# Norms without shift: the product with the root moves to GpSimd in odd rows, and the weight into the copy and the low half

## The reference, cut to what matters

```python
def rms_norm(x, g):
    xf = x.astype(jnp.float32)
    y = xf * lax.rsqrt(jnp.mean(xf * xf, axis=-1, keepdims=True) + RMS_EPS)
    return y.astype(x.dtype) * g.astype(x.dtype)
...
h = h + dilated_attention_mixer(rms_norm(h, attn_norm[j]), positions, ...)
h = h + swiglu(rms_norm(h, ffn_norm[i]), ffn_w_in[i], ffn_w_out[i])
h = h + mlstm_mixer(rms_norm(h, mlstm_norm[j]), ...)
```

## Time and profile before

| | |
|---|---|
| median of 3 runs | 2984.96 us |
| lowest, highest | 2984.22, 2986.41 us |
| profiled execution | span 2983.2 us, 43523 instructions |
| busy | TensorE 97%, VectorE 67%, ScalarE 40%, GpSimd 12% |
| mean granted TensorE clock | 0.992 of full |

### The profile page before, as it was taken

The page is one execution under the profiler, slowest core; times in us unless marked ns, Lnnn a source line. Parts: engine busy times, 40 slices in busy tenths (PEclk is TensorE's granted clock), DMA queues, the critical chain, the costliest instruction groups (busy, mean ns, idle before and its releaser), DMA issues.

```text
span 2983.2 us, 43523 instructions
## 1 busy us (share of the span) xinstructions
PE 2888.3 (97%) x18080; PEld 2524.0 (85%) x18080; DVE 2004.9 (67%) x3284; ACT 1202.5 (40%) x1993; POOL 349.9 (12%) x542
## 2 busy tenths in 40 slices
PE   7999999989999999999999999999999999998998
PEld 7999998889997778888866888888888888877898
DVE  7776887668655557777745677777777777554665
ACT  5444544554444444223314533223243222443543
POOL 0000001000022220000131100011010000243000
PEclk9999999999999999999999999999999999999999
DMA  7544675347655424555473255553535555465453
GB/s 241 168 159 152 216 229 190 120 161 234 204 125 81 72 64 147 157 167 169 132 190 107 80 168 163 169 165 124 170 120 164 168 163 169 117 96 86 142 184 128
DMA packets 362277, 451.85 MB, mean 151 GB/s; under 512 B 12656, under 2 KB 332432, under 8 KB 362080
## 3 DMA queue, kind: packets, MB, share of 16 engines
q1 hardware_dynamic: 326976, 329.83, 34.1%
q0 software_dynamic: 34944, 118.65, 16.9%
q10 hardware_dynamic: 160, 0.59, 0.1%
HBM read 438.60 MB, written 1.05 MB: 147 GB/s over the span
## 4 chain that ended last, share of the span: by engine, by line
PE 79%; DVE 12%; ACT 5%; DMA 2%; issue 1%; POOL 1%; DVEq 0%; SPq 0%; ACTq 0%
PE ps L1352 23%; PE ps L1354 23%; PE ps L1353 23%; DVE lo L1932 4%; PE ps L1530 1%; ACT hi L1602 1%; PE ps L1373 1%; PE ps L1517 1%; DVE NB L1963 1%; DMA NB<-in_na_rpb 1%; PE ps L1375 1%; PE ps L1374 1%; DVE MX L2008 1%; PE ps L1505 1%; DVE XN L1969 1%
## 5 line engine op out<-in xcount | busy, mean ns | idle before, releaser
L1352 PE MATMUL ps<-XN,hi 128*128 128x256 f32 (+1 forms) x3184 | 1048.8, 329 | 32.9 <-DVE XN L1949 9.9
L1353 PE MATMUL ps<-XN,hi 128*128 128x256 f32 (+1 forms) x3184 | 1029.9, 323 | 0.0
L1354 PE MATMUL ps<-XN,lo 128*128 128x256 f32 (+1 forms) x3184 | 1029.6, 323 | 0.0
L1932 DVE TENSOR_TENSOR lo<-raw,hi 128x1024 fp32r<-128x1024 f32 (+1 forms) x626 | 739.2, 1221 | 250.6 <-ACT hi L1602 245.4
L1602 ACT ACTIVATE hi<-raw 128x1024 fp32r<-128x1024 f32 (+1 forms) x626 | 620.6, 1040 | 443.5 <-PE ps L1354 440.7
L1352 PEld LDWEIGHTS ps<-XN,hi 128*128 128x128 f32 x3184 | 610.6, 192 | 106.6 <-issue 17.4
L1354 PEld LDWEIGHTS ps<-XN,lo 128*128 128x128 f32 x3184 | 610.8, 192 | 46.1
L1353 PEld LDWEIGHTS ps<-XN,hi 128*128 128x128 f32 x3184 | 611.2, 192 | 44.8
L2008 DVE CUSTOM_DVE_ANT_0 MX<-MW,C 128x1024 bf16<-128x1024 f32 x384 | 477.2, 1243 | 130.7 <-DMA MW<-in_mod_w 123.8
L1352 PE MATMUL ps<-H,hi 128*128 128x512 f32 (+1 forms) x1072 | 380.2, 355 | 0.0
L1353 PE MATMUL ps<-H,hi 128*128 128x512 f32 (+1 forms) x1072 | 379.7, 354 | 0.0
(11 more groups left out here) (255 smaller groups left out, 3194.8 us busy)
## 6 DMA issues: line engine op xcount, KB each, us to landing
raw<-in_mlp_w SPq DMA_DIRECT2D x128, 1024.0 KB, 5.3
MW<-in_mod_w POOLq DMA_DIRECT2D x192, 512.0 KB, 3.8
raw<-in_ffn_w_in SPq DMA_DIRECT2D x44, 1024.0 KB, 5.4
raw<-in_attn_w_in SPq DMA_DIRECT2D x36, 1024.0 KB, 4.9
raw<-in_na_wqkv SPq DMA_DIRECT2D x24, 1024.0 KB, 5.0
raw<-in_ffn_w_out SPq DMA_DIRECT2D x16, 1024.0 KB, 5.1
raw<-in_mlstm_w_in SPq DMA_DIRECT2D x12, 1024.0 KB, 5.1
raw<-in_cv_w SPq DMA_DIRECT2D x12, 1024.0 KB, 6.2
```

The costliest lines, as they stand in the source:

```text
L1352: e.matmul(out, whi, xhi, start=first, stop=False)
L1353: e.matmul(out, whi, xlo, start=False, stop=False)
L1354: i = e.matmul(out, wlo, xhi, start=False, stop=last)
L1932: e.tensor_tensor(lo[:, a:b], raw[:, a:b], hi[:, a:b].bitcast(F32), ALU.subtract).then_inc(*low.says(("lo", j, i), ("spent", j) if i else ...
```

## The change

In a norm without shift, tiles with odd k take another way. GpSimd multiplies X by RS alone, into the same buffer; ScalarE's copy takes the weight as its scale; VectorE's low half becomes a scalar_tensor_tensor, NB \* weight - XN high. Tiles with even k, and all norms with a shift, stay.

```diff
+def by_gpsimd(k, shift):
+
+    return shift is None and k % 2 == 1
...
# scalar
     def scale(s, k, n, gain, shift, used):
         tmp = (m.TN, m.SQ)[k % 4 // 2][:, k % 2, :]
         w.wait_ge(used)
+        if by_gpsimd(k, shift):
+            w.wait_ge(("scaled", s, k, 0), "params")
+            e.activation(m.XN[:, 0, k, 0:n], tmp[:, 0:n], ACT.Copy, scale=gain_of(m, gain, k, 0)).then_inc(
+                *act.says(("xnhi", s, k, 0)))
+            return
...
# vector
     def scale(s, k, n, gain, shift, unit):
         tmp = (m.TN, m.SQ)[k % 4 // 2][:, k % 2, :]
+        if by_gpsimd(k, shift):
+            return
...
-    def rest(s, k, n, shift):
+    def rest(s, k, n, gain, shift):
         tmp = (m.TN, m.SQ)[k % 4 // 2][:, k % 2, :]
+        if by_gpsimd(k, shift):
+            w.wait_ge(("xnhi", s, k, 0))
+            e.scalar_tensor_tensor(out=m.XN[:, 1, k, 0:n], in0=tmp[:, 0:n], scalar=gain_of(m, gain, k, 0),
+                                   in1=m.XN[:, 0, k, 0:n].bitcast(F32), op0=ALU.mult, op1=ALU.subtract).then_inc(
+                *dve.says(("xn", s, k)))
+            return
...
# gpsimd
+    def scale(s, k, n, gain, shift, unit):
+        if by_gpsimd(k, shift):
+            w.wait_ge(("x", 0, 0), ("x", 0, 4), ("rstd", s), ("xn", s, k - 4) if k >= 4 else None)
+            e.tensor_tensor(m.NB[:, k % 4, 0:S], m.X[:, k, 0:S], m.RS[:, 0:S], ALU.mult).then_inc(
+                *pool.says(("scaled", s, k, 0)))
```

More of the change, by code:

```diff
@@ L485, in first_norm @@
             if k:
-                self.do("rest", s, k - 1, S, None)
+                self.do("rest", s, k - 1, S, gain, None)
             if k == 2:
@@ L509, in norm @@
             if k >= ahead:
-                self.do("rest", s, k - ahead, n, shift)
+                self.do("rest", s, k - ahead, n, gain, shift)
         self.sq_user = [("xn", s, KT - 2), ("xn", s, KT - 1)]
@@ L2435, in sc_pads @@
             e.memset(m.UP[:, :, :, :, a:a + 1], 0.0).then_inc(*pool.says("sc_pads"))
-    go_through(p, {"mod_load": mod_load, "square": square, "square_part": square_part, "context": context, "ml_pads": ml_pads, "na_zero": na_zero,
+    go_through(p, {"mod_load": mod_load, "scale": scale, "square": square, "square_part": square_part, "context": context, "ml_pads": ml_pads, "na_zero": na_zero,
                    "na_table": na_table, "cv_pads": cv_pads, "cv_spread": cv_spread, "cv_spread_one": cv_spread_one,
```

## The result

The changed kernel took 2988.96 us (median of 18 runs, 2983.55 to 2994.49), the kernel before 2984.23 in the same series (18 runs, 2983.47 to 2988.91). The ratio is 1.0014, interval 1.0008 to 1.0021: slower, by less than 0.2%, but above the predicted range of 2982.3 to 2988.0. Three more series of the same kernel, made for the experiments, gave 2986.98 (beside 2985.51), 2987.89 and 2986.22 (both beside 2985.08), ratios 1.0009, 1.0005 and 1.0001. The differences of the means, +4.6, +2.6, +2.0 and +0.2 us, weighted by the 18, 11, 11 and 11 runs, make **+2.7 us**; +0.35 was forecast. The runs of the changed kernel also lie further apart (standard deviation 3.3 to 4.2 us, before 1.5 to 2.3). An explanation has to yield some 2.4 us on the average, more in one execution than in another.

A forecast was written before the change was run, and what follows sets the result against it. TensorE, busy 2888.3 of 2983.2 us, bounds the kernel, so only its standstill can be won. First norm -1.2, norms two to four +0.5, +0.55, +0.5 sum to +0.35 us: 2985.3 us, range 2982.3 to 2988.0.

The forecast's parts named there:

- The start, -1.2: First norm: GpSimd's first load moves behind its products, weights come earlier, TensorE takes up k=2 1.2 us earlier.
- the prediction's other bound (-2.6): First norm: -2.6 us with everything good.
- The turns: Norms: VectorE and GpSimd alternate; a waiting GpSimd product needs 0.60 us after its release, a waiting VectorE instruction 0.28.
- (a): Norms: no taking of turns, -0.25, -0.4, -0.25 in two to four, -1.7 in the first; 2982.4 us; chance 0.10.
- (c): Norms: whole instructions exclude each other, 0.62 us more per norm, 0.1 in the first; 2987.3 us; chance 0.08.
- h at 0.50: Odd tiles of the norms: ScalarE's copy with a weight from memory takes 0.50 us, between 0.42 and 0.51.
- Norms two to four, +0.5, +0.55, +0.5: TensorE later by 0.5 us at norms two and four, 0.55 at norm three, through VectorE and GpSimd alternating.
- rival (d): Norm three: longer, more broken waits lower the clock, 1.8 us per stretch; one stretch gives 2987.1 us; chance 0.12.
- The sign that the prediction gave for (d): Norm three: a granted clock below 0.6 for longer than 4 us would show the lowered clock.
- Its size for one stretch, 2987.1: Norm three: one more low-clock stretch, 17 matmuls where 32 fit, costs 1.8 us and gives 2987.1 us.
- The argument of gapless running: Norms two and four: TensorE runs without a gap once started, held against a lowered clock.

The follow-up runs named there:

- e1: The kernel before, with only GpSimd's first conditions load moved behind the first norm: 2983.74 beside 2986.03 us, ratio 0.9992.
- e2: The changed kernel, with its first conditions load issued ahead of the GpSimd products: 2989.80 beside 2986.03 us, ratio 1.0015.
- e5: The changed kernel, with the odd tiles' product back on VectorE and the conditions load at its old place: 2985.28 beside 2985.51 us, ratio 0.9999.
- e4: The kernel before, with the change only in norms two to four and the load in front: 2988.85 beside 2986.03 us, ratio 1.0010.
- e10: The changed kernel without the change in norm three (the mLSTM's): 2984.61 beside 2984.92 us, ratio 1.0002.
- e8: The changed kernel, with all eight tiles of norms two to four on GpSimd, first norm as before, load in front: 2993.23 beside 2984.92 us, ratio 1.0029.
- e7: The kernel before, with one more ScalarE pass over the root in norms two to four: 2986.29 us, ratio 1.0003.
- e3: The kernel before, with only the first norm changed and the load behind its products: 2984.73 beside 2986.03 us, ratio 1.0001.
- e9: The kernel before, with only norm three (the mLSTM's) changed: 2986.40 beside 2984.92 us, ratio 1.0005.
- e6: The kernel before, with eight small ScalarE passes ahead of the first weight split: 2986.05 beside 2985.51 us, ratio 1.0003.
- e1_again: A repetition of the kernel before with only the first conditions load behind the first norm: 2983.52 beside 2985.08 us, ratio 0.9995.

## Why the prediction was wrong

- **The start, -1.2: right, and more was to be had.** First split forecast at 10.2, measured 10.40; k = 2 at 17.9, measured 17.99; GpSimd's load near 19 us, measured 19.49. e1 and e2 show from both sides that it is the load. The traces gain 1.3 to 2.9 us, since the clock also rises earlier, as the prediction's other bound (-2.6) had it: the four profiles of the changed kernel have -2.4, so this term was 1.2 too small, and in the sum it hid a part of what the clock took later. Two readings on the way are off and change nothing: the load had 44% of the bytes at 5 to 8 us, not a third, and the sum of squares ended 0.9 us before the first hi, not 0.8.
- **The turns: the steps right, the first pair the other way round.** A p ends 0.59 us behind the VectorE instruction before it, an s or r 0.28 behind a p, and from r0 on each end is within 0.03 us of the forecast: last r 6.77, measured 6.74; wait of TensorE 3.3, measured 3.35. Before r0 the forecast had s0 end at 0.51 and p1 at 1.11; measured are p1 at 0.80 and s0 at 1.08. That r0's end agrees even so (2.27, measured 2.28) is luck: the first of the five instructions ended 0.29 us later than forecast, and the four behind it took 0.28 us less, since r0 stood behind s2 and not behind p3. Out are (a), which wants s and r at their free length everywhere, and (c), which has r0 end at 2.89. The Trainium skill, "SBUF — State Buffer", section "Who interferes with whom", says that a VectorE instruction with two SBUF inputs contends with a GpSimd instruction that reads SBUF, and calls the port pair that they share an exclusive lock. This trace agrees that they contend (s of 1.05 and 0.94 us instead of 0.48), and shows two s and two p in 1.92 us, where 2 x 0.48 + 2 x 0.74 = 2.44 would stand one behind another.
- **h at 0.50: right.** 494 ns against 417 in even rows, and hidden (e5). The Trainium skill, "ScalarE: Activation LUTs", section "What ACT_TABLE_LOAD costs", adds about 93 ns for each operand in memory; these rows have 77. The whole duration is 494, where an estimate by the formula of that section, 186 + 93 + 0.833 x 256, gives 492.
- **Norms two to four, +0.5, +0.55, +0.5: right as far as they go.** The table has +0.46, +0.56 and +0.44 in the first profile, where these stretches have no more low clock than before.
- **The step that failed: the sum has no term for more time at the low clock.** It passes the rest of the kernel on one to one behind each norm. The prediction put that term off as rival (d), "the longer and more broken waits lower it for one more stretch", with a chance of 0.12, with norm three as the place, and with the argument that TensorE runs without a gap in norms two and four. The runs show in its place: the granted clock of the changed kernel is 0.9906 over 51 runs instead of 0.9917, which is 3.3 us. In the profiles, 5.1 us more of low clock lie between 290 and 670 us on the mean, of which about 0.85 at norm two, 1.7 at norm three, 1.7 in the mLSTM behind it and 0.85 at norm four (second profile: norms two and three and the mLSTM; third: norm four; fourth: norm three and the mLSTM; the first has less than the kernel before), and 3.4 us more lie after 670 us. The sign that the prediction gave for (d), a clock below 0.6 for longer than 4 us at norm three, came in the second and fourth profile (6.8 us). Its size for one stretch, 2987.1, is 2.1 above the median it started from, beside a measured 2.7; that this is near is chance, since 1.2 us more at the start hid a part. The argument of gapless running fell too: in the second profile the stretch at norm two is 6.8 us long instead of 3.4.
- What is shown: the turns cost what they were priced at (traces of the changed kernel, e4 and e10); the rest of the loss is time at the low clock, with the same busy time and fewer matmuls (windows of e4, of the second profile and of e8; the clocks of all runs); it comes with the products on GpSimd (changed kernel, e2) and not with the load's place (e1), the longer copy and low half (e5), or a root that is late by the same time (e7: clock 0.9921).
- What is open: how the products bring the low clock about. That the position of the work against the clock's rises and falls decides it is only argued. For it speak the order of the four profiles and e3, whose profile has a longer low stretch at norm three with nothing changed there; e10 and e9, with a part of the turns and 20.5 and 17.1 us of low time, show that a norm held up by turns doesn't always bring it. Which norm does it is open as well: e3, e4, e9 and e10 by themselves are not clear of the noise in their clocks. In the first profile the low clock past 670 us comes more often than in the first profile of the kernel before, at 926, 2680 and 2725 us; two of these places, 2679 and 2723 us, are in e7's profile too, and one, 2679, in the second profile of the kernel before. How much of the first series' 4.6 us over the mean of 2.7 was chance stays open too.

## What to carry to other kernels

Before work is moved to an idle engine, look at what that engine's queue already holds: here the gain came from pushing back a load of 0.52 MB that nobody needed before 44 us, and one changed wait gives that without the rest. What two engines cost each other at memory could be priced from one place in a trace to some 0.03 us a step, but not who goes first. Work that is moved can also cost clock, here 3.3 us beside 1.5 of waiting, and not only where it stands. A mean granted clock over many runs shows that better than any one profile. A difference of 0.1% should be timed in several series against itself before it is believed.

## What the runs showed of the hardware that I had not expected

- The granted clock stands as 1.00 in the first 18 to 23 us of the windows, while matmuls start 0.21 us apart (1.2 GHz) and later 0.12 apart (2.4 GHz): there, read the pace.
- The same program goes from 1.2 to 2.4 GHz at 17.90 to 19.33 us in four executions, and spends 17 to 34 us at the low clock between 290 and 670 us.
- A start that was 2.3 us late cost 0.75 us at 100 us (e6), one that was 1.1 us early was worth 2.4 (changed kernel), and one that was 1.3 us early 1.3 (e1_again, clock up at 22.3 us) or 2.9 (e1, at 16.9): how much of the start is kept depends on when the clock rises.
- The kernel before repeats its trace within 0.1 us up to 2000 us; the four executions of the changed kernel are up to 4.9 us apart by 670 us.
